# Second attention of an encoder: score products with 128 rows, the probabilities' low part behind the logits, and the first queries' weights behind the first keys'

## What is computed

```python
s = jnp.einsum('bnqhgd,bnjhd->bhgnqj', q, kb)      # 128 queries against 3 blocks of 128 keys
s = jnp.where(mask, s + bias, lowest)              # shared relative bias, |i - j| <= 128
m = jnp.maximum(jnp.max(s, axis=-1), sink)
p = jnp.exp(s - m)
p = p / (jnp.sum(p, axis=-1) + jnp.exp(sink - m))
o = jnp.einsum('bhgnqj,bnjhd->bnqhgd', p, vb)      # then the output projection
```

## Time and profile before

| | before |
|---|---|
| median of three runs | 1148.82 us (1148.69 to 1149.16) |
| the profiled execution | 1148.75 us |
| its span, first to last instruction | 1147.1 us |
| TensorE busy | 1136.0 us, 99% |
| VectorE busy | 630.4 us, 55% |
| ScalarE busy | 504.8 us, 44% |
| GpSimd busy | 138.0 us, 12% |
| mean granted clock of TensorE | 0.997 |

### The profile page before, as it was taken

One profiled execution on the slowest core, in us unless ns is written; L12 is line 12 of the kernel. 1 busy time (PEld: TensorE's weight loads), 2 busy tenths in 40 slices (PEclk: granted clock), 3 DMA queues, 4 the chain that ended last, 5 costly groups with the idle time before them and its releaser, 6 DMA issues.

```text
span 1147.1 us, 16682 instructions
## 1 busy us (share of the span) xinstructions
PE 1136.0 (99%) x5644; PEld 937.1 (82%) x5644; DVE 630.4 (55%) x1020; ACT 504.8 (44%) x908; POOL 138.0 (12%) x239
## 2 busy tenths in 40 slices
PE   9999999999999999999999999999999999999997
PEld 6888888888888888888887788888888888888886
DVE  7788887764442234444345778766444223444333
ACT  6777677553431223333334666645343122333221
POOL 6544341330000000000000322100000000000000
PEclk9999999999999999999999999999999999999998
DMA  6322331343223222322222212123322332232222
GB/s 225 97 89 92 91 91 55 96 120 105 91 92 102 100 91 92 107 94 90 93 91 92 51 53 59 52 74 95 107 91 92 100 102 92 91 107 95 91 92 92
DMA packets 34291, 106.98 MB, mean 93 GB/s; under 512 B 5760, under 2 KB 8096, under 8 KB 34256
## 3 DMA queue, kind: packets, MB, share of 16 engines
q1 hardware_dynamic: 29344, 98.61, 26.2%
q0 software_dynamic: 4768, 7.90, 2.9%
q10 hardware_dynamic: 144, 0.02, 0.0%
HBM read 103.84 MB, written 2.67 MB: 93 GB/s over the span
## 4 chain that ended last, share of the span: by engine, by line
PE 98%; DVE 1%; DMA 0%; ACT 0%; SPq 0%; issue 0%; DVEq 0%; ACTq 0%
PE acc L400 29%; PE acc L402 28%; PE acc L401 28%; PE s_ps L504 3%; PE om_ps L538 2%; PE pt_ps L708 2%; PE om_ps L562 1%; PE om_ps L534 1%; PE pt_ps L525 1%; PE om_ps L494 1%; PE s_ps L400 1%; PE s_ps L401 1%; PE s_ps L402 1%; DMA w_raw<-in_wstream 0%; PE om_ps L547 0%; DVE x_res L1304 0%
## 5 line engine op out<-in xcount | busy, mean ns | idle before, releaser
L802 ACT CAST w_hi<-w_raw 128x1024 fp32r<-128x1024 f32 x179 | 188.1, 1051 | 401.5 <-PE acc L402 395.1
L400 PE MATMUL acc<-h_hi,w_hi 128*128 128x512 f32 x792 | 318.4, 402 | 0.7 <-DVE w_lo L1086 0.7
L401 PE MATMUL acc<-h_lo,w_hi 128*128 128x512 f32 x792 | 308.9, 390 | 0.0
L402 PE MATMUL acc<-h_hi,w_lo 128*128 128x512 f32 x792 | 308.8, 390 | 0.0
L1086 DVE TENSOR_TENSOR w_lo<-w_raw,w_hi 128x1024 fp32r<-128x1024 f32 x177 | 217.9, 1231 | 143.7 <-ACT w_hi L802 143.0
L400 PE MATMUL acc<-u_hi,w_hi 128*128 128x512 f32 (+1 forms) x624 | 241.2, 387 | 0.0
L401 PE MATMUL acc<-u_lo,w_hi 128*128 128x512 f32 (+1 forms) x624 | 239.5, 384 | 0.0
L402 PE MATMUL acc<-u_hi,w_lo 128*128 128x512 f32 (+1 forms) x624 | 239.5, 384 | 0.0
L400 PEld LDWEIGHTS acc<-h_hi,w_hi 128*128 128x128 f32 x792 | 148.8, 188 | 37.5 <-issue 4.8
L402 PEld LDWEIGHTS acc<-h_hi,w_lo 128*128 128x128 f32 x792 | 148.7, 188 | 31.7
L401 PEld LDWEIGHTS acc<-h_lo,w_hi 128*128 128x128 f32 x792 | 149.1, 188 | 28.5 <-issue 0.7
(11 more groups left out here) (141 smaller groups left out, 1000.1 us busy)
## 6 DMA issues: line engine op xcount, KB each, us to landing
w_raw<-in_wstream SPq DMA_DIRECT2D x180, 512.0 KB, 3.3
bias_pairs<-rpb_reversed POOLq DMA_DIRECT2D x64, 62.0 KB, 2.4
bias_pairs<-t_shifted POOLq DMA_DIRECT2D x64, 48.0 KB, 2.2
x_res<-in_xT SPq DMA_DIRECT2D x8, 256.0 KB, 5.6
out_y<-x_res SPq DMA_DIRECT2D x8, 128.0 KB, 1.8
out_y<-x_res SPq DMA_DIRECT2D x4, 256.0 KB, 2.3
t_shifted<-vT POOLq DMA_DIRECT2D x16, 31.0 KB, 2.1
mask<-in_mask POOLq DMA_DIRECT2D x1, 64.0 KB, 5.5
```

What stands on the lines that cost most here:

```text
L400: nc.tensor.matmul(dst, a[0], b[0], start=start, stop=False)
L401: nc.tensor.matmul(dst, a[0], b[1], start=False, stop=False)
L402: return nc.tensor.matmul(dst, a[1], b[0], start=False, stop=stop)
L802: nc.scalar.copy(w_hi[:, c.odd, :], w_raw[:, c.odd, :]).then_inc(w_hi_made, 1)
```

## The change

The diff has four parts.
1. **Scores.** `head_products` isn't used here any more. For each head the queries' high and low parts are stacked in one tile of 128 partitions (`q_stack`), the keys' high part is there twice, above and below (`k_stack_hi`), and so is their low part (`k_stack_lo`). A score is two products of 128 rows, stacked queries by doubled high keys and by doubled low keys, so four parts' products are summed in place of three. The stacks are made by casts and subtractions on 64 partitions: two and two for the queries of a pair (`queries_high`, `queries_low`), four casts on ScalarE, two subtractions on VectorE and two copies on GpSimd for a key tile (`keys_high`, `keys_low`, `keys_doubled`).
2. **Order in a step.** On VectorE `sw_pt_low` comes directly behind the logits (in slots 1 and 3 behind `sw_o_low`, which moves there), ahead of the sum, the scaling and the queries' low part; the sum of slot 1 stays in it, and the scaling moves from slot 2 to slot 1, the queries' low part from slot 3 to slot 2. On ScalarE the outputs' high part moves behind the second exponential. On TensorE `transpose_o` moves to slots 0 and 2, between the first dense part and the scores.
3. **Before the steps.** The queries of pair 0 are the second chunk of the stage (`SW_FIRST`), their tile is made second, and the scores of unit 0 stand behind the fifth chunk and no longer in the sixth; its logits stand ahead of `v_low`.
4. **Behind the steps** the last `transpose_o`, `sw_o_low` and `sw_pt_low` change places.

```diff
+SW_FIRST = [0, 4, 1, 2, 3, 5]
+        def q_stack(odd, hh):
+            return (u_lo if hh else u_hi)[:, 8 + odd, :]
+        def k_stack_hi(kv, hh):
+            return (k_lo if hh else k_hi)[:, kv, :]
+        def k_stack_lo(kv, hh):
+            return u_hi[:, 10 + 2 * kv + hh, :]
...
+            for kv in range(2):
+                pool.wait_ge(tile_split, TI_SW + 2 * kv + 1)
+                for hh in range(2):
+                    nc.gpsimd.tensor_copy(k_stack_lo(kv, hh)[HEAD_ROWS[1 - hh], :],
+                                          f32(k_stack_lo(kv, hh)[HEAD_ROWS[hh], :])).then_inc(keys_doubled, 1)
+                    pool.wait_ge(keys_doubled, 2 * kv + hh + 1)
...
-                head_products(lambda hh: s_ps[:, hh, 0:nb * P], (8 + p.odd, slice(P * n, P * (n + 1))),
-                              (p.odd, slice(P * kb, P * (kb + nb)))).then_inc(scores_done, 1)
+                for hh in range(2):
+                    queries, keys = q_stack(p.odd, hh)[:, P * n:P * (n + 1)], slice(P * kb, P * (kb + nb))
+                    nc.tensor.matmul(s_ps[:, hh, 0:nb * P], queries, k_stack_hi(p.odd, hh)[:, keys], start=True, stop=False)
+                    ins = nc.tensor.matmul(s_ps[:, hh, 0:nb * P], queries, k_stack_lo(p.odd, hh)[:, keys], start=False,
+                                           stop=True)
+                ins.then_inc(scores_done, 1)
...
                     dense_part(2 * n)
+                    if n == 0 and before:
+                        transpose_o(p * 2 + (HEADS - 2), sw_bank(0))
+                    if n == 2 and before:
+                        transpose_o(p * 2 + (HEADS - 1), sw_bank(1))
                     if n < 3 or last != 8:
                         sw_scores(*sw_unit_by(p, n, 1))
                     dense_part(2 * n + 1)
-                    if n == 1 and before:
-                        transpose_o(p * 2 + (HEADS - 1), sw_bank(1))
-                    if n == 3:
-                        transpose_o(p * 2 + HEADS, sw_bank(0))
...
+            part(At(CH_SW + 3), At(GR_SW + 3), h_tile, range(4))
             sw_v_blocks(0)
-            part(At(CH_SW + 3), At(GR_SW + 3), h_tile, ALL)
+            part(At(CH_SW + 3), At(GR_SW + 3), h_tile, range(4, 8))
             part(At(CH_SW + 4), At(GR_SW + 4), h_tile, ALL)
+            sw_scores(At(0), 0)
+            part(At(CH_SW + 5), At(GR_SW + 5), h_tile, range(2))
             sw_v_blocks(1)
-            part(At(CH_SW + 5), At(GR_SW + 5), h_tile, range(4))
+            part(At(CH_SW + 5), At(GR_SW + 5), h_tile, range(2, 4))
             pe.wait_ge(v_split, UNITS_NA + 2)
-            sw_scores(At(0), 0)
...
+            def queries_high(m):
+                first = m.a == 0 and m.b == 0
+                act.wait_ge(acc_taken, GR_SW + 2 if first else (m + (GR_SW + 5)).v)
+                src = scaled[:, 1 if first else m.odd, :]
+                nc.scalar.copy(q_stack(m.odd, 0)[TOP, :], src[TOP, :])
+                nc.scalar.copy(q_stack(m.odd, 1)[BOTTOM, :], src[BOTTOM, :]).then_inc(tile_hi, 1)
...
                     sw_exp(p, n, 0)
-                    if n == 0 and before:
-                        sw_o_high(p + -1, 0)
-                    if n == 2 and before:
-                        sw_o_high(p + -1, 1)
                     if before or n >= 1:
                         sw_pt_high(*sw_unit_by(p, n, -1))
                     sw_exp(p, n, 1)
                     if n % 2 == 1:
                         sw_sinks(p, n // 2)
+                    if n == 0 and before:
+                        sw_o_high(p + -1, 0)
                     if n == 2 and dense:
-                        tile_high(m + (GR_SW + 4), m + (TI_SW + 2), u_hi[:, 8 + m.odd, :])
+                        queries_high(m)
+                    if n == 2 and before:
+                        sw_o_high(p + -1, 1)
                     if n == 3:
                         split_weights(m + (CH_SW + 6))
...
             def queries_low(m):
-                tile_low(m + (TI_SW + 2), u_lo[:, 8 + m.odd, :], u_hi[:, 8 + m.odd, :])
+                first = m.a == 0 and m.b == 0
+                dve.wait_ge(tile_hi, TI_SW + 2 if first else (m + (TI_SW + 3)).v)
+                src = scaled[:, 1 if first else m.odd, :]
+                for hh in range(2):
+                    own, other = HEAD_ROWS[hh], HEAD_ROWS[1 - hh]
+                    ins = nc.vector.tensor_tensor(q_stack(m.odd, hh)[other, :], src[own, :],
+                                                  f32(q_stack(m.odd, hh)[own, :]), ALU.subtract)
+                ins.then_inc(tile_split, 1)
...
                 for n in range(4):
-                    sw_logits(p, n)
-                    if n == 0 and before:
+                    if before or n >= 1:
+                        sw_logits(p, n)
+                    if n == 1 and before:
                         sw_o_low(p + -1, 0)
-                    if n == 1 and before:
-                        sw_o_sum(p + -1, 1)
-                    if n == 2 and before:
+                    if n == 3 and before:
                         sw_o_low(p + -1, 1)
-                    if n == 2 and dense:
-                        scale_queries(m)
-                    if n == 3 and dense:
-                        queries_low(m)
-                    if n == 3:
-                        sw_o_sum(p, 0)
                     if before or n >= 1:
                         sw_pt_low(*sw_unit_by(p, n, -1))
                     if n == 0:
                         split_weights(m + (CH_SW + 5))
+                    if n == 1 and before:
+                        sw_o_sum(p + -1, 1)
+                    if n == 1 and dense:
+                        scale_queries(m)
+                    if n == 2 and dense:
+                        queries_low(m)
+                    if n == 3:
+                        sw_o_sum(p, 0)
```

More of the change, by code:

```diff
@@ L286, in _ @@
             load_weights(At(3))
-            with sp.Fori(2, CHUNKS // 2) as i:
+            with sp.Fori(2, CH_SW // 2) as i:
+                for n in range(2):
+                    load_weights(At(n, 2, i))
+            for n, place in enumerate(SW_FIRST):
+                load_weights(At(CH_SW + n), CH_SW + place)
+            with sp.Fori((CH_SW + len(SW_FIRST)) // 2, CHUNKS // 2) as i:
                 for n in range(2):
@@ L694, in sw_scores @@
                 if n == 0:
-                    pe.wait_ge(tile_split, (p + (TI_SW + 3)).v)
+                    first = p.a == 0 and p.b == 0
+                    pe.wait_ge(tile_split, TI_SW + 2 if first else (p + (TI_SW + 3)).v)
+                    pe.wait_ge(keys_doubled, 2 if first else 4)
                 pe.wait_ge(logits_made, sw_unit(p, n).v)
                 kb, nb = SW_BLOCKS[n]
-                head_products(lambda hh: s_ps[:, hh, 0:nb * P], (8 + p.odd, slice(P * n, P * (n + 1))),
-                              (p.odd, slice(P * kb, P * (kb + nb)))).then_inc(scores_done, 1)
+                for hh in range(2):
[4 more added lines that the diff above has]
+                ins.then_inc(scores_done, 1)
             def sw_transpose(p, n):
@@ L856, in tile_high, with keys_high @@
                 nc.scalar.copy(dst, src).then_inc(tile_hi, 1)
+            def queries_high(m):
[4 more added lines that the diff above has]
+                nc.scalar.copy(q_stack(m.odd, 1)[BOTTOM, :], src[BOTTOM, :]).then_inc(tile_hi, 1)
+            def keys_high(kv):
+                act.wait_ge(acc_taken, GR_SW + 3 * kv + 1)
+                src = scaled[:, 0, :]
+                for hh in range(2):
+                    for half in HEAD_ROWS:
+                        ins = nc.scalar.copy(k_stack_hi(kv, hh)[half, :], src[HEAD_ROWS[hh], :])
+                ins.then_inc(tile_hi, 1)
             def v_high(batch, dst):
@@ L1405, in queries_low, with keys_low @@
             def queries_low(m):
-                tile_low(m + (TI_SW + 2), u_lo[:, 8 + m.odd, :], u_hi[:, 8 + m.odd, :])
+                first = m.a == 0 and m.b == 0
+                dve.wait_ge(tile_hi, TI_SW + 2 if first else (m + (TI_SW + 3)).v)
+                src = scaled[:, 1 if first else m.odd, :]
+                for hh in range(2):
+                    own, other = HEAD_ROWS[hh], HEAD_ROWS[1 - hh]
+                    ins = nc.vector.tensor_tensor(q_stack(m.odd, hh)[other, :], src[own, :],
+                                                  f32(q_stack(m.odd, hh)[own, :]), ALU.subtract)
+                ins.then_inc(tile_split, 1)
+            def keys_low(kv):
+                dve.wait_ge(tile_hi, TI_SW + 2 * kv + 1)
+                for hh in range(2):
+                    own = HEAD_ROWS[hh]
+                    ins = nc.vector.tensor_tensor(k_stack_lo(kv, hh)[own, :], scaled[own, 0, :],
+                                                  f32(k_stack_hi(kv, hh)[own, :]), ALU.subtract)
+                ins.then_inc(tile_split, 1)
             def sw_step(m, before=True, dense=True):
```

43 lines of the change are left out of this document (25 added, 18 removed).

## The result

| | before | after |
|---|---|---|
| median | 1148.82 us (1148.69 to 1149.16) | 1159.99 us (1159.76 to 1160.16) |
| the profiled execution | 1148.75 us | 1159.99 us |
| its span | 1147.1 us | 1158.3 us |

The ratio of after to before is 1.0097, with a 95% interval of 1.0083 to 1.0111: slower by 1.0%, 11.2 us between the two profiled executions. The prediction was 1158.4 us in a range of 1151.5 to 1164.

What follows compares the result with a forecast made beforehand. TensorE set 15.94 us a pair before; after, a closed chain through VectorE and ScalarE takes 17.41. 1148.75 + 8.8 (six steps) - 0.8 + 0.5 + 0.9 (ends) = 1158.1, taken as 1158.4 us; range 1151.5 to 1164.

Steps and rivals of the forecast that it cites:

- The scores: TensorE's score unit as four 128-row passes: 0.47 us for two blocks, 0.69 for three, saving 1.07 a pair.
- TensorE stays the bound: Rival: the chain fits under TensorE's 14.87 us a pair, so the time is 1139.9; chance 0.08.
- the 0.41: Part of a two-block score unit's 0.76 us on TensorE, laid to changes between 128-row and 64-row work.
- The halves: Queries' operands as two 64-partition instructions each: 0.62 us apiece on ScalarE, 0.70 on VectorE, no cheaper than whole ones.
- The slots: Four pieces of a pair's chain through VectorE and ScalarE: 3.39, 4.57, 5.24 and 4.21, together 17.41 us.
- TensorE's waits: TensorE stands about 2.5 us a pair, ahead of the scores and the values, nearly all in slots 2 and 3.
- The loop's turn: Sequencer's work at a loop's turn, partly no longer covered by a running low part: 0.3 us in all.
- The ends: Outside the six full steps: -0.8 us until the first values, +0.5 in the first step, +0.9 in the last.
- Costed at nothing: Keys' casts and subtractions, GpSimd's four copies and the moved chunk of queries: no time added.
- Halves cost half: Rival: slot 2's query halves take 0.7 and 0.7 us, chain 16.2, time about 1150; chance 0.05.
- only the passes count: Rival: TensorE binds and loses 0.12 or 0.17 us a unit, 4.6 in all, 1153.4; chance 0.03.
- The longer chain: Rival: waits between engines met today become real, 0.5 us a pair more, 1162; chance 0.10.

Runs made afterwards that it cites:

- best1: Changed kernel with new ScalarE and VectorE orders (high part first in slots 0 to 2, scaling ahead of low part in slot 2); 1144.11 us, ratio 0.9958.
- best3: best1 plus the first head's high products (all but the last) issued ahead of the low-part wait, and VectorE's loop written out; 1142.57 us, ratio 0.9943.
- high_first: Changed kernel with ScalarE's high part of unit n-1 moved ahead of the first exponential of unit n; 1149.63 us, ratio 1.0006.
- old_order: Changed kernel, its products and halves kept, with all three engines' orders within a step and behind the last as before; 1149.12 us, ratio 1.0001.
- order_only: Kernel before, with 64-row products and whole queries, given only the new orders of the three engines; 1154.27 us, ratio 1.0045.
- values_early: Changed kernel with the first head's high products (all but the last) issued ahead of the wait for the low part; 1159.55 us, ratio 1.0091.
- unrolled: Changed kernel with VectorE's loop over steps 2 to 7 written out as six steps; 1158.73 us, ratio 1.0093.

## Why the prediction was right, and where it was off

The runs as a table of products and operands against the order, in us:

| | order of before | order of after | order of best1 |
|---|---|---|---|
| 64-row products, whole queries | 1148.9 | 1154.3 | 1149.1 |
| 128-row products, whole queries | not run | 1154.7 | not run |
| 128-row products, queries by halves | 1149.1 | 1160.0 | 1144.1 |

Down the middle column, the order costs 5.4 us (against the 1148.9 of the same chip), the products 0.4, which is within the scatter of the two, and the halves 5.3. The right column has the products' gain, 5.0 us net of what the halves may cost there.

- **The scores.** Predicted 0.47 and 0.69 us a unit. Both come where the scores stand right behind a dense pass and wait for nothing: 0.47 in after (630.84 to 631.31) and 0.70. Behind the output transposes or behind a wait the first pass takes longer, and a unit takes 0.56 to 0.58 or 0.79. What failed is the step "four 128-row passes of 0.12" (and of 0.17): it left out that a first pass there doesn't have its weights loaded ahead. In best3, where TensorE sets the pace, a pair's units take 0.56, 0.57, 0.71 and 0.79, which saves 0.75 a pair and not 1.07. By that TensorE alone would take 15.19 a pair, not 14.87; best3 has 15.07 to 15.19. It changed nothing in after, where TensorE waits anyway, but "TensorE stays the bound" was priced too low by it: near 1142.5 and not 1139.9.
- **The rule on tiling.** The dense pass behind the scores has its follower at 0.22 again. That part of the 0.41 was the change of shape, so the weighing against "TensorEngine Tiling (Array Packing)" of the Trainium skill, Theoretical Speedup, holds: three passes side by side with changes of shape cost 0.76, four alone 0.47 behind a dense pass and 0.56 behind transposes.
- **The halves.** Predicted 0.62 and 0.62 on ScalarE, 0.70 and 0.70 on VectorE. Measured as starts: 0.61 (667.16 to 667.77) and 0.65 to VectorE's start; 0.70 and 0.72. The sum of 2.66 is 2.68 in the trace. The hold that "VectorE: DVE Perf Modes" of the Trainium skill gives, Two Vector instructions with no wait between them, is met: 0.70 from one half to the next, the whole of its duration.
- **The slots.** 3.39, 4.57, 5.24 and 4.21 were predicted, 3.37, 4.54, 5.24 and 4.80 came, and 4.19 for the last with the loop written out. The mechanism is shown from three sides: undone on ScalarE (high_first), undone everywhere (old_order), and done alone (order_only).
- **TensorE's waits.** "Some 2.5 us a pair at the values and the scores": 22.5 us of waits at the weight loads in eight pairs, 2.8 a pair, at these two places. That they are an effect is shown by values_early.
- **The loop's turn.** This is the term that was mis-sized. The prediction set 0.3 us for all turns. Each of the two ways back costs 0.61 and each other step of the loop 0.12, 1.7 us in the six pairs, and the way in 0.3 more. Without the loop six pairs are 8.4 us longer than before (104.02 against 95.62), where 6 x 1.47 = 8.8 was forecast.
- **The ends.** Predicted -0.8, +0.5 and +0.9, together +0.6; measured -0.63, +1.65 and +0.07, +1.1. The first values are 0.17 later than forecast. The stretch up to the logits of pair 1 loses 1.15 more. Of that, 0.3 is the way into the loop: unrolled has +1.34. And slot 1 of the first step is 3.76 long (625.74 to 629.50), where the pieces without an output sum give 3.10. Without that sum ahead of it, the scaling, which was moved into this slot, waits 0.58 for TensorE's new queries (VectorE's row at 628.89); in old_order and best1, which scale in slot 2, the same slot takes 2.56. The +0.9 of the tail doesn't follow from the prediction's own pieces: slots 1 and 2 without new queries are 3.97 + 2.98 = 6.95 by them, they came as 6.90 (748.36 to 755.26), and before they took 7.04. So one end lost 1.15 more than forecast and the other 0.83 less. That they nearly cancel is luck; no run changed an end alone.
- **Costed at nothing.** The keys' halves, GpSimd's copies and the moved chunk: TensorE's waits between 585 and 765 us in after name none of them, and in old_order, which has all three, the first values come 0.5 us earlier than before.

With these the sum closes: 10.14 for six pairs, where 8.8 was forecast, and 1.1 for the ends, where 0.6 was. That is 11.2 against 9.4, or 9.7 with the turn as priced. Of the 1.6 us by which the median lies above the forecast, the loop in the six pairs is 1.4 and the ends 0.5, and the chain, priced 0.4 too high, takes some of it back.

The rivals: "TensorE stays the bound" (1139.9) fell, its 2.5 us a pair are there as waits. "Halves cost half" (1150) fell with the rows of the halves, 0.61 and 0.69 us each, and "only the passes count" (1153.4) with TensorE's row of scores, 0.70 for three blocks where it needs 1.1. "The longer chain" (1162) was the nearest, but its reason was not what happened in the full steps: no slot of them is longer by waits that were met before; the excess is the loop. Only in the first step did such a wait become real, the 0.58 of the scaling. What the forecast didn't see is how near the good order lay: with ScalarE's high part ahead of the exponential the chain opens (high_first), and in best1 the products pay.

Why do high_first and old_order end so close to before, and not below it? Their pairs are longer than TensorE's: from the first to the last of the seven slot-1 logits high_first takes 96.86 us (641.36 to 738.22) and old_order 96.49 (641.42 to 737.91), 1.24 and 0.87 more than before's 95.62, and the earlier first values (628.46 and 628.75 against 629.24) give 0.8 and 0.5 back. What the halves alone cost in these orders was not run.

## What to carry to other kernels

Cut the period into slots at one instruction that recurs and sum the pieces along the path through all engines, before asking who is busiest: an engine that wins 1 us a period gains nothing when a closed chain through two others is longer. When an operation is moved close behind the one before it, look at what used to run in the wait and whether the partner engine, whose order wasn't touched, still feeds it in time; here one exchange on ScalarE was worth 10 us. A wait on the bounding engine may be the end of the chain: moving it (values_early) tells in one run whether it is worth anything.

## What was not expected of the hardware

- VectorE's loop costs time when no running instruction covers it: 0.61 us at each way back to its start in after, 0.12 between the two steps of a round, 0.30 on the way in (rows of 0.22 and 0.52 us "issue"). In before, where a low part ran over it, no row on VectorE waits on "issue" in these steps.
- A first 128-row product of 256 columns takes 0.20 us behind short transposes and 0.22 behind a wait, against 0.12 behind a dense pass or in a row.
- An instruction of 64 partitions and 512 columns takes what one of 128 partitions does, to 0.01 us: 0.61 on ScalarE, 0.69 on VectorE. The prediction had this as its likelier bound only.
